# A condition's modulation vectors on GpSimd: from scaled weight rows summed by TensorE to products with the condition's row, halved down to one number

## What is computed

```python
mod = (c @ w_ada[l] + b_ada[l]).reshape(B, N_MOD, D_MODEL)        # N_MOD = 9
sh1, sc1, g1, sh2, sc2, g2, sh3, sc3, g3 = [mod[:, None, i] for i in range(N_MOD)]
h = modulate(rmsnorm_2(x, ffn1_norm[l]), sh1, sc1)                # h * (1 + scale) + shift
x = x + 0.5 * (1 + g1) * swiglu_2(h, ...)
h = modulate(rmsnorm_2(x, mix_norm[l]), sh2, sc2)
x = x + (1 + g2) * hybrid_mixer(h, ...)
h = modulate(rmsnorm_2(x, ffn2_norm[l]), sh3, sc3)
x = x + 0.5 * (1 + g3) * swiglu_2(h, ...)
```

## Time and profile before

| what | value |
|---|---|
| median of three runs | 2768.28 us |
| the profiled execution, own time | 2765.86 us |
| its span, first to last instruction | 2763.9 us |
| PE busy | 2700.8 us (98%) |
| DVE busy | 1881.0 us (68%) |
| ACT busy | 1245.1 us (45%) |
| POOL busy | 628.1 us (23%) |
| chain that ended last | PE 86%, DVE 7%, ACT 3%, issue 2%, DMA 1%, POOL 1% |
| mean granted TensorE clock | 0.993 of full |

### The profile page before, as it was taken

How to read it: one execution, slowest core, us unless ns; L and a number is a source line. 1 busy time by engine, 2 the same in 40 slices (tenths; PEclk the granted TensorE clock), 3 DMA queues, 4 the chain that set the end, 5 groups by cost and what they waited for, 6 DMA issues and landing times.

```text
span 2763.9 us, 43691 instructions
## 1 busy us (share of the span) xinstructions
PE 2700.8 (98%) x17285; PEld 2397.9 (87%) x17285; DVE 1881.0 (68%) x2051; ACT 1245.1 (45%) x1594; POOL 628.1 (23%) x519
## 2 busy tenths in 40 slices
PE   8999999999999999999999999999999999999998
PEld 8987789999979999998799888888888878888887
DVE  6885765588777886665766657666766667665765
ACT  4443444444444444444444445344434454445443
POOL 5863400078536851000100100000000420000000
PEclk9999999999999999999999999999999999999999
DMA  8754145567527766533455526435643436533552
GB/s 300 253 206 156 47 168 203 185 250 257 196 82 262 262 227 236 182 129 131 141 201 182 168 95 233 184 128 198 235 183 122 154 134 229 199 131 107 214 204 91
DMA packets 127001, 502.04 MB, mean 182 GB/s; under 512 B 11168, under 2 KB 12480, under 8 KB 93488
## 3 DMA queue, kind: packets, MB, share of 16 engines
q1 hardware_dynamic: 112768, 450.40, 45.6%
q0 software_dynamic: 14128, 50.18, 5.2%
HBM read 499.48 MB, written 1.06 MB: 181 GB/s over the span
## 4 chain that ended last, share of the span: by engine, by line
PE 86%; DVE 7%; ACT 3%; issue 2%; DMA 1%; POOL 1%; SPq 0%; DVEq 0%; ACTq 0%; POOLq 0%
PE duo L1264 8%; PE duo L1249 8%; PE duo L1250 8%; PE duo L1247 7%; PE duo L1394 7%; PE duo L1398 7%; PE duo L1402 7%; PE duo L1263 4%; PE duo L1757 4%; PE duo L1758 3%; PE duo L1762 3%; DVE in_lo L366 2%; DVE down_lo L366 1%; ACT in_hi L359 1%; PE duo L2302 1%
## 5 line engine op out<-in xcount | busy, mean ns | idle before, releaser
L366 DVE TENSOR_TENSOR in_lo<-ring_in,in_hi 128x2048 fp32r<-128x2048 f32 x295 | 698.9, 2369 | 346.3 <-ACT in_hi L359 346.1
L359 ACT CAST in_hi<-ring_in 128x2048 fp32r<-128x2048 f32 (+1 forms) x293 | 555.8, 1897 | 246.5 <-PE duo L1762 133.1
L366 DVE TENSOR_TENSOR down_lo<-ring_down,down_hi 128x1024 fp32r<-128x1024 f32 (+1 forms) x196 | 346.8, 1769 | 29.2 <-ACT down_hi L359 29.2
L1511 ACT CAST hid_hi<-act 128x256 fp32r<-128x256 f32 (+1 forms) x196 | 93.3, 476 | 418.2 <-DVE act L1597 347.9
L359 ACT CAST down_hi<-ring_down 128x1024 fp32r<-128x1024 f32 (+1 forms) x196 | 260.5, 1329 | 44.2 <-PE duo L1402 44.2
L1394 PE MATMUL duo<-down_hi,hid_hi 128*128 128x512 f32 x928 | 242.5, 393 | 6.9 <-ACT hid_hi L1511 6.9
L1247 PE MATMUL duo<-feat,in_hi 128*128 128x512 f32 x1024 | 246.6, 392 | 0.0
L1249 PE MATMUL duo<-feat,in_hi 128*128 128x256 f32 (+1 forms) x1015 | 241.8, 281 | 3.6 <-ACT in_hi L359 3.5
L1250 PE MATMUL duo<-feat,in_hi 128*128 128x256 f32 (+1 forms) x1015 | 240.5, 280 | 0.0
L1398 PE MATMUL duo<-down_lo,hid_hi 128*128 128x512 f32 x928 | 239.3, 389 | 0.0
L1402 PE MATMUL duo<-down_hi,hid_lo 128*128 128x512 f32 x928 | 239.0, 389 | 0.0
(11 more groups left out here) (532 smaller groups left out, 5619.1 us busy)
## 6 DMA issues: line engine op xcount, KB each, us to landing
ring_in<-in_ffn_in SPq DMA_DIRECT2D x196, 1024.0 KB, 6.6
ring_down<-in_ffn_down SPq DMA_DIRECT2D x132, 512.0 KB, 3.7
ring_down<-in_ffn_down SPq DMA_DIRECT2D x64, 1024.0 KB, 4.9
mod_w<-in_w_ada POOLq DMA_DIRECT2D x72, 512.0 KB, 5.1
ring_in<-in_sb_w_qkv SPq DMA_DIRECT2D x24, 1024.0 KB, 5.2
ring_in<-in_conv_w_in SPq DMA_DIRECT2D x12, 1024.0 KB, 5.1
ring_in<-in_gla_w_in SPq DMA_DIRECT2D x12, 1024.0 KB, 5.1
ring_in<-in_nsa_w_in SPq DMA_DIRECT2D x10, 1024.0 KB, 5.1
```

The lines of the kernel that those rows point to most:

```text
L359: act.copy(hi[:, s, 0:n], raw[:, s, 0:n]).then_inc(hi_ready.sem, 1)
L366: dve.tensor_tensor(lo[:, s, 0:n], raw[:, s, 0:n], hi[:, s, 0:n].bitcast(F32), ALU.subtract).then_inc(lo_ready.sem, 1)
```

## The change

The weights are laid out anew on the host: a chunk now holds 128 output features in the partitions and all 1024 input features along the row (72 chunks for nine vectors). The condition's row is spread over all partitions by a DMA at the head of each part. POOL takes chunks in pairs, 1 MB a load and 12 pairs a part: one product of the pair (128 x 2 x 1024) with the row, then five additions that each halve the rows (to 512, 256, 128, 64 and at last 32 numbers, the last into `mod_parts`), each link waiting for the one before it. At the end of a part five more halvings over all 24 chunks at once give one number per output feature, the bias is added, and POOL finishes scale and gate itself. The sum across partitions falls away with `ModSpread` and its PE, ACT and DVE instructions; in their places ACT, DVE and POOL only wait for the part (`ModDone`). The gate row goes to DRAM from 128 partitions with 8 numbers each instead of from one partition.

```diff
 class Modulation:
+    WIDTH = 32
-        self.sum, self.w = k.mod_sum, k.mod_w
+        self.row, self.w = k.mod_row, (k.mod_pair[:, :, :], k.mod_w[:, :, :])
         self.columns = k.sb("mod_columns", 9, KC)
-        self.gate_rows = k.sb("mod_gates", D)
+        self.bias = k.sb("mod_bias", 9, KC)[:, :, :]
+        self.parts = k.sb("mod_parts", 3 * KC, self.WIDTH)[:, :, :]
...
 class ModPart(Stage):
+    PAIRS = 3 * KC // 2
...
-        v, c = 3 * self.branch + i // 9, i % 9
-        if c < KC:
-            pool.dma_start(mod.w[:, s, :], k.dram["w_ada_2"][c * P:(c + 1) * P, v * D:(v + 1) * D]).then_inc(mod.landed[s].sem, 16)
-        else:
-            pool.dma_start(mod.w[0:1, s, :], k.dram["b_ada_2"][0:1, v * D:(v + 1) * D]).then_inc(mod.landed[s].sem, 16)
+        chunk = 3 * KC * self.branch + 2 * i
+        pool.dma_start(mod.w[s], k.dram["w_ada_2"][chunk:chunk + 2].rearrange("c p n -> p c n")).then_inc(mod.landed[s].sem, 16)
+
+    def _halve(self, pool, out, rows, n):
+        return pool.tensor_tensor(out, rows[:, :, 0:n], rows[:, :, n:2 * n], ALU.add)
...
+        pool.dma_start(mod.row, k.dram["rows"][c_2:c_2 + 1, :].partition_broadcast(P)).then_inc(mod.row_landed.sem, 16)
         self._load(pool, 0)
-        for i in range(27):
-            if i + 1 < 27:
+        if b == 0:
+            pool.dma_start(mod.bias.rearrange("p v c -> p (v c)"), k.dram["b_ada_2"]).then_inc(mod.bias_landed.sem, 16)
+        pool.wait_ge(mod.row_landed.sem, 16 * (b + 1))
+        row = mod.row.unsqueeze(1).broadcast_to([P, 2, D])
+        for i in range(self.PAIRS):
+            if i + 1 < self.PAIRS:
                 self._load(pool, i + 1)
...
-            if c == 0:
-                pool.tensor_scalar(total, mod.w[:, s, :], k.col("c_2", c), 0.0, ALU.mult, ALU.add).then_inc(mod.used.sem, 1)
-            elif c < KC:
-                k.pool_link(pool, pool.tensor_scalar(mod.w[:, s, :], mod.w[:, s, :], k.col("c_2", c), 0.0, ALU.mult, ALU.add))
-                pool.wait_ge(mod.used.sem, g)
-                pool.tensor_tensor(total, total, mod.w[:, s, :], ALU.add).then_inc(mod.used.sem, 1)
...
+            k.pool_link(pool, pool.tensor_tensor(mod.w[s], mod.w[s], row, ALU.mult))
+            n = D // 2
+            while n > mod.WIDTH:
+                k.pool_link(pool, self._halve(pool, mod.w[s][:, :, 0:n], mod.w[s], n))
+                n //= 2
+            self._halve(pool, mod.parts[:, 2 * i:2 * i + 2, :], mod.w[s], n).then_inc(mod.used.sem, 1)
...
+        n = mod.WIDTH // 2
+        while n > 1:
+            k.pool_link(pool, self._halve(pool, mod.parts[:, :, 0:n], mod.parts, n))
+            n //= 2
+        all_three = mod.columns[:, 3 * b:3 * b + 3, :]
+        k.pool_link(pool, self._halve(pool, all_three.rearrange("p v c -> p (v c)").unsqueeze(2), mod.parts, 1))
+        k.pool_link(pool, pool.tensor_tensor(all_three, all_three, mod.bias[:, 3 * b:3 * b + 3, :], ALU.add))
...
+        k.pool_link(pool, pool.tensor_scalar(gate, gate, half, half, ALU.mult, ALU.add))
+        k.pool_link(pool, pool.tensor_scalar(scale, scale, 1.0, 1.0, ALU.mult, ALU.add))
+        pool.tensor_tensor(scale, scale, k.col(self.gain, 0, KC), ALU.mult).then_inc(mod.summed.sem, 1)
-class ModSpread:
...
+class ModDone:
+    def wait(self, eng):
+        eng.wait_ge(self.mod.summed.sem, self.branch + 1)
...
-        self.spread.scalar(act)
+        self.made.wait(act)
-        self.spread.vector(dve)
+        self.made.wait(dve)
-        wait_all(pe, [(self.spread.mod.kept.sem, 3)])
```

More of the change, by code:

```diff
@@ L1656, with __init__ @@
     regions = REGIONS
-    def __init__(self, core, before, w, how, dst=None, spread=None, gate=None, order=None):
+    def __init__(self, core, before, w, how, dst=None, made=None, gate=None, order=None):
         super().__init__(core, before)
         self.feat_hi, self.feat_lo = before.feat_hi, before.feat_lo
-        self.w, self.how, self.dst, self.spread, self.gate = core.dram[w], how, dst, spread, gate
+        self.w, self.how, self.dst, self.made, self.gate = core.dram[w], how, dst, made, gate
         n = self.w.shape[1]
@@ L2934, with __init__ @@
     ROPED = {0: (0, 4), 2: (512, 8), 3: (1024, 8), 4: (1536, 8)}
-    def __init__(self, core, before, spread):
-        super().__init__(core, before, "nsa_w_in", "store", dst=core.proj, spread=spread, order=self.FIRST)
+    def __init__(self, core, before, made):
+        super().__init__(core, before, "nsa_w_in", "store", dst=core.proj, made=made, order=self.FIRST)
         k = core
@@ L3191, with __init__ @@
     ROPED = {0: (D, 2), 1: (0, 8), 2: (BLK, 8)}
-    def __init__(self, core, before, spread):
-        super().__init__(core, before, "swa_w_in", "store", dst=core.proj, spread=spread, order=self.FIRST)
+    def __init__(self, core, before, made):
+        super().__init__(core, before, "swa_w_in", "store", dst=core.proj, made=made, order=self.FIRST)
         k = core
@@ L3418, with __init__ @@
 class ModPart(Stage):
-    def __init__(self, core, before, mod, branch):
+    PAIRS = 3 * KC // 2
+    def __init__(self, core, before, mod, branch, gain):
         super().__init__(core, before)
-        self.mod, self.branch = mod, branch
+        self.mod, self.branch, self.gain = mod, branch, gain
         self.l0 = mod.loads
-        mod.loads += 27
-        self.s0 = mod.summed.plan(1)
+        mod.loads += self.PAIRS
     def _load(self, pool, i):
@@ L4700, in glu @@
         if part is not None:
-            plan.append(ModPart(k, feed, mod, part))
+            plan.append(ModPart(k, feed, mod, part, gains[part]))
         plan.append(FeedForward(k, feed, name[0], name[1], True, "half_rstd", free))
@@ L4799, in down_units, with modulation_chunks @@
     return np.ascontiguousarray(w.reshape(n, chunks, P, D).transpose(0, 2, 1, 3)).reshape(n, P, chunks * D)
+def modulation_chunks(w, bias):
+    by_chunk, by_partition = np.arange(D).reshape(KC, P), np.arange(D).reshape(P, KC).T
+    rows = np.concatenate([v * D + (by_partition if v % 3 == 2 else by_chunk) for v in range(9)])
+    return np.ascontiguousarray(w.T[rows.reshape(-1)]).reshape(9 * KC, P, D), np.ascontiguousarray(bias[rows].T)
 def arrays_of(a):
```

96 lines of the change are left out of this document (30 added, 66 removed).

## The result

The changed kernel takes 2958.91 us (median of four runs, 2957.17 to 2959.83), the kernel before 2767.93 us: ratio 1.0698, 95% interval 1.0681 to 1.0716, 191 us slower. I had forecast 2878 us, slower, with 2812 to 2925 as the range. The direction and the place were right; the size was not: 2959 lies outside the range, with 191 us of cost where I had 110.

The account below looks back on a forecast made before the run. PE was taken to bound the feed-forward stages, with POOL's work hidden beside it; 3 x 40 - 10 = +110 us on 2765.86 gives 2876, as the median of runs 2878 us, range 2812 to 2925.

Parts of the forecast that it names:

- PE bounds the stages: Feed-forward stages: PE is busy 185.00 us of 185 without modulation work and 184.25 us with it.
- Prices of POOL's instructions: POOL's new work: 0.15 us plus 2.2 ns a number, 9.8 us a pair, 121 us a part, 10% either way.
- DMA costs nothing: Loads of the parts: each pair's load has the whole preceding pair, over 10 us, to land, so no cost.
- a pair covers two units when they alternate: DVE's loop beside a part: six POOL instructions a pair against three DVE turns a unit; 62 to 73 us a part.
- 28 us of slack a part: Feed-forward units: DVE's loop takes 7.03 us, PE 8.32, leaving 1.29 us a unit, 28 us over 22 units.
- The lower bound of 19 us a part: Stages with parts: 208 us of exclusive DVE and POOL work in 185 plus 4 us, at least 19 us over.
- The upper bound of 52: Stages with parts: a part costs at most 45 us and 10% on prices, 52 us.
- One-input instructions yield: DVE and POOL sharing: POOL's two-input instructions take turns with DVE, its one-input ones let DVE pass.
- The removal gives 10 us: Sum across partitions gone: 6.1 us at most in NSA, 2.9 in SWA, 1.1 in branch 2; bounds 0 to 20.
- Rival 3, the clock falls: PE beside the parts: its waits lower the granted clock to 1.2 GHz, 25 us more, 2903 us; chance 12%.
- Rivals 1 and 2: 1: POOL still hides in DVE's gaps, 2758 us, 11%. 2: DVE keeps its turn, POOL ends late, 2818 us, 12%.
- What would show it: Profile signs: `down_lo` over 3 us, PE waiting 2 to 3 us, three stages 40 us longer, POOL over 100 us busier.

Follow-up runs that it names:

- late loads: The changed kernel with each pair's load issued behind the first halving of the pair before, instead of ahead of its product: 2921.85 us.
- part 2 of the single chunks: The last part in the changed kernel remade with one chunk at a time, each load issued behind the first halving of the chunk before: 2927.57 us whole.
- one-input run: The changed kernel with the pair's product as a tensor_scalar of the same size instead of a tensor_tensor (modulation vectors wrong): 2867.32 us.
- loads-only kernel: The changed kernel with loads, closing halvings and waits kept, but the pairs' products and halvings replaced by a write of zeros: 2762.74 us, ratio 0.9986.
- run with PE's work cut: The changed kernel without PE's products of the low halves of the down-projection weights, in every feed-forward stage: 2793.74 us.
- ten issues less: The changed kernel with only the first two pairs of each part loaded and all twelve products and halvings made on these buffers: 2917.16 us.
- first pacing: The changed kernel with one more wait per pair, its product starting only after DVE's low half of the down-projection weights of unit 20 i / 11: 2891.85 us.
- second pacing: The changed kernel with the product of pair i held until behind unit 2 i (at most 21), plus idle PE products in NSA: 2881.63 us, ratio 1.0427.
- single chunks: The changed kernel with one chunk of 128 x 1024 at a time instead of a pair, 24 loads and products a part: 2914.63 us.

## Why the prediction was off, point by point

- *PE bounds the stages, POOL's work is hidden today, DVE and POOL shut each other out*: right. Away with the arithmetic, away with the cost.
- *Prices of POOL's instructions*: right. The product of 2048 took 4.60 (4.66 forecast), the last halving 0.32 (0.29). *DMA costs nothing*: right for the time, and the 14.8 us of waiting for the row, over three parts, lengthened nothing.
- *"a pair covers two units when they alternate", 5.2 to 6.1 us a pair*: **this step failed.** I took each POOL instruction as one turn and let DVE have a turn between any two. But only those that meet one of DVE's three count: the short halvings follow one another while DVE reads PSUM, and so all of a pair fits into one unit, stretched to 14.1 us. It costs DVE 4.9 + 2.2 us, 7.1, as the product meets no gap: it comes with `in_lo` every time. Twelve pairs are 85 us, not 67.
- *28 us of slack a part*: the second half of the failure. The slack lies in all 22 units, but pairs stand only in twelve: 12 x 1.29 = 15, and five units behind them run at 7.0 us and regain 5 x 1.3 = 6.6. 85 - 22 = 63 us, where 63.6, 60.3 and some 68 were measured. The lower bound of 19 us a part was never undercut, but it is no true floor: the lengths that it adds up overlap by some 0.7 us a unit (13.0 us with late loads, 8.7 in part 2 of the single chunks), which makes it some 9 us too high (an estimate, 12 x 0.77). Only a POOL that is held back comes near it; free running it takes all of the resource at once and leaves it idle later.
- *The upper bound of 52*: it had the prices' 10% in it and nothing for order. That is why the range missed.
- *One-input instructions yield*: right for `in_lo` and `down_lo` at 604.99, wrong as a rule, as the one-input run shows. The trace of before already had seven cases against it, which I overlooked, such as an `in_lo` of 3.37 us at 72.29 beside a one-input product at its full speed (1.13 us) at 72.39. The rule in the Trainium skill (SBUF — State Buffer, "Who interferes with whom") that the shared pair is held for the whole instruction fits these rows to within some 0.1 us an instruction. That whoever issues first gets it does not fit the starts that the trace shows: the product of 701.95 has it against the `in_lo` of 701.54.
- *The removal gives 10 us*: wrong; in the changed kernel NSA is 5.0 us longer and SWA 0.6 shorter, and the loads-only kernel as a whole is 3 us under before. NSA turned its 6 into a wait for a load and a fall of the clock (+5.0). In SWA the transposes did come 3.0 us sooner behind 1/rms (13.7 to 10.7), but the clock now fell twice for 3.4 us, at 895 and 922, where it had fallen once; what else took the gain back was not traced. With POOL's arithmetic gone altogether and the clock kept up in NSA, the kernel is 9 us under before (2756.9 against 2765.9 us on the same chip); more was not seen here.
- *Rival 3, the clock falls*: it fell 27 times beside the parts, for 3.4 or 6.8 us, at no cost, as the run with PE's work cut shows. *Rivals 1 and 2*: neither held; POOL was done 63.5 us or more before its 1/rms was wanted.
- *What would show it*: PE's waits of up to 3.0 us before L1395 in each unit with a pair, as said; `down_lo` in the mean 3.37 us beside the pairs of part 1, one of 5.63; but `in_lo`, 6.0 us in the mean, carries the larger part. POOL's busy time rose by 83.5 us, not over 100, because the products before were long by waiting (3.59 us at 604.99).

## What to carry to other kernels

Work that is hidden beside a bound engine is priced by the unit, not by the stage: ask how much of it lands in one unit, in which order, and what is left of the slack in the units where it does not stand. Where it comes in bursts, pace it with one wait on the loop's own semaphore before making it smaller, and see which neighbour its largest piece lands on: one chunk cost 9.6 - 8.3 = 1.3 us a unit beside `in_lo` and 0.4 just before `hid_lo`. Taking work off an engine that then waits for a load gains nothing, and it may cost the clock.

## What the hardware did that I had not expected

- A VectorE instruction with both inputs in SBUF is overtaken by a GpSimd one that starts a little after it, when a DMA issue of POOL's queue ends right before the latter (idle time under 0.05 us). In the changed kernel 28 products start 0.40 to 0.51 us behind `in_lo` and it waits for all of them; so it does for 27 of the one-input form, at 0.43 to 0.54 us, and for seven of the kernel before, at 0.09 to 0.43 us:

```profile
72.29 3.37 DVE L366 TENSOR_TENSOR in_lo<-ring_in,in_hi 128x2048 fp32r<-128x2048 f32 x1 [0.52 <-ACT in_hi L359]
```

```profile
72.39 1.13 POOL L3456 TENSOR_SCALAR mod_w<-mod_w,cols 128x1024 f32<-128x1024 f32 x1
```

Where POOL's instruction started 0.66 us or later behind `in_lo`, in the kernel before, it waited and `in_lo` took 2.28 us; so it did once at 0.28 us, for the sum of the one-partition bias row. Released by a landing instead, products waited at 0.04 us (904.40, kernel before), 0.14 us (961.29, ten issues less), 0.35 us (943.49, first pacing), 0.37 us (616.94, second pacing), and 0.77 us in the run with late loads:

```profile
653.47 5.99 POOL L3451 TENSOR_TENSOR mod_w<-mod_w,mod_row 128x2048 f32<-128x2048 f32 x1 [3.58 <-DMA mod_w<-in_w_ada]
```

The issue alone does no harm: in the loads-only run `in_lo` starts at 29.24, inside an issue of 0.70 us, and takes 2.29 us. So the distance alone does not decide, and the issue alone neither: right behind an issue and up to 0.54 us late, POOL went first in 62 of 63 cases of these three kernels. Why it is so stays open.
- GpSimd's `tensor_scalar` takes 1.99 us for 2048 numbers, its `tensor_tensor` 4.60.
- The granted clock fell in nearly every unit beside the pairs, to half for 3.4 us at least, where PE was busy some 40 of 54 us; with single chunks, PE busy 8.3 of 9.6 us in each unit, it did not fall once between 30 and 210 us. Busy time by stretch, the changed kernel, then single chunks:

```profile
703.00:757.00 54.00, 40.34 (x240) 35.70 (x240) 45.73 (x20) 12.64 (x15) 51.48 (x27) 0.87 0.49 180
```

```profile
30.00:210.00 180.00, 166.85 (x1162) 149.16 (x1161) 160.77 (x96) 69.36 (x77) 164.84 (x128) 1.00 0.60 221
```
